# Staging x1's first half inside the attention loop and joining attention and mixing in one block (GLA and pooling trunk, one Trainium2 core)

## What is computed

```python
# layer 0: gated linear attention, 4 heads, chunks of 64 tokens
h = x @ w_in                      # q, k, v, g, low-rank gate
o = intra-chunk attention + q-decayed state of the chunks before
o = rmsnorm(o) * norm_w * silu(g)
x1 = layernorm(alpha * x + o @ w_out)
# layer 1: causal pooling mixer, width 2048, windows 2, 4, 8, 16
u, z = split(x1 @ w_in)
m = (windowed mean of u - u) @ w_grp + b, scaled
y = (m * silu(z)) @ w_out
out = layernorm(alpha * x1 + y)
```

## Time and profile before

| | |
|---|---|
| executions shown | 1974.26 us median of 3 (1969.22, 1974.26, 1974.47) |
| the profiled execution | 1964.6 us; its span 1962.9 us, 1.7 us lie around the span |
| mean granted clock | 0.981 |
| PE busy | 1861.6 us (95%) |
| PE weight loads | 1535.0 us (78%) |
| DVE busy | 1398.3 us (71%) |
| ACT busy | 852.5 us (43%) |
| POOL busy | 598.2 us (30%) |
| DMA | 171 GB/s over the span |

### The profile page before, as it was taken

One profiled execution on the slowest core, in us unless ns is written; L12 is line 12 of the kernel. 1 busy time (PEld: TensorE's weight loads), 2 busy tenths in 40 slices (PEclk: granted clock), 3 DMA queues, 4 the chain that ended last, 5 costly groups with the idle time before them and its releaser, 6 DMA issues.

```text
span 1962.9 us, 24653 instructions
## 1 busy us (share of the span) xinstructions
PE 1861.6 (95%) x8688; PEld 1535.0 (78%) x8688; DVE 1398.3 (71%) x1769; ACT 852.5 (43%) x1323; POOL 598.2 (30%) x380
## 2 busy tenths in 40 slices
PE   8989999999999699999679999999999998999997
PEld 7878887886788588888558888887888786887786
DVE  3454555778667678787666788768899967546997
ACT  4554445657555434333444444344333344224221
POOL 1322231332221000000145665405566532323330
PEclk9999999999999799999879999999999999999999
DMA  8967572557365645443413544242546326556442
GB/s 286 321 200 266 195 248 97 152 141 247 90 171 179 239 145 188 171 162 138 171 43 116 170 150 144 98 172 75 178 170 221 140 93 215 208 192 257 161 151 97
DMA packets 259725, 336.43 MB, mean 171 GB/s; under 512 B 18208, under 2 KB 187936, under 8 KB 255904
## 3 DMA queue, kind: packets, MB, share of 16 engines
q1 hardware_dynamic: 259616, 335.02, 50.9%
HBM read 218.58 MB, written 116.39 MB: 171 GB/s over the span
## 4 chain that ended last, share of the span: by engine, by line
PE 38%; DVE 7%; issue 4%; ACT 1%; POOL 0%; DVEq 0%; ACTq 0%; POOLq 0%
PE banks L200 13%; PE banks L202 12%; PE banks L201 12%; DVE m_w_lo L2520 2%; DVE m_x_lo L2534 1%; DVE m_win_a L2550 1%; ACT m_x_hi L2310 0%; DVE m_res L2633 0%; DVE m_win_b L2550 0%; DVE m_x_lo L2512 0%; PE banks L2203 0%; PE banks L2250 0%; DVE m_win_b L2566 0%; DVE m_res L2617 0%; DVE m_x_lo L2494 0%
## 5 line engine op out<-in xcount | busy, mean ns | idle before, releaser
L200 PE MATMUL banks<-m_x_hi,m_w_hi 128*128 128x512 f32 x1320 | 517.7, 392 | 12.6 <-DVE m_z L2596 6.6
L201 PE MATMUL banks<-m_x_lo,m_w_hi 128*128 128x512 f32 x1320 | 515.1, 390 | 0.0
L202 PE MATMUL banks<-m_x_hi,m_w_lo 128*128 128x512 f32 x1320 | 514.9, 390 | 0.0
L200 PEld LDWEIGHTS banks<-m_x_hi,m_w_hi 128*128 128x128 f32 x1320 | 248.8, 188 | 68.7 <-DVE m_w_lo L2520 10.6
L202 PEld LDWEIGHTS banks<-m_x_hi,m_w_lo 128*128 128x128 f32 x1320 | 248.7, 188 | 52.1
L201 PEld LDWEIGHTS banks<-m_x_lo,m_w_hi 128*128 128x128 f32 x1320 | 248.6, 188 | 51.8 <-issue 0.7
L200 PE MATMUL banks<-b_hi,h_w_hi 128*128 128x512 f32 x656 | 257.9, 393 | 6.1 <-issue 4.5
L202 PE MATMUL banks<-b_hi,h_w_lo 128*128 128x512 f32 x656 | 256.3, 391 | 0.0
L201 PE MATMUL banks<-b_lo,h_w_hi 128*128 128x512 f32 x656 | 256.0, 390 | 0.0
L2298 ACT ACTIVATE m_w_hi<-m_s 128x512 fp32r<-128x512 f32 x184 | 115.5, 629 | 186.2 <-PE banks L202 166.0
L2436 POOL TENSOR_TENSOR m_s<-pair_raw 128x512 f32<-128x512 f32 x24 | 46.7, 1945 | 469.0 <-POOLq L1512 365.1
(11 more groups left out here) (276 smaller groups left out, 3363.2 us busy)
## 6 DMA issues: line engine op xcount, KB each, us to landing
b_raw<-x_in SPq DMA_DIRECT2D x14, 1024.0 KB, 9.8
p_in<-in_pool_w_in SPq DMA_DIRECT2D x32, 256.0 KB, 5.7
w_fused<-p_out SPq DMA_DIRECT2D x32, 256.0 KB, 3.5
x_in<-h_terms SPq DMA_DIRECT2D x8, 1024.0 KB, 4.3
v_tiles<-h_v_out SPq DMA_DIRECT2D x16, 512.0 KB, 4.0
in_raw<-in_gla_w_in SPq DMA_DIRECT2D x16, 512.0 KB, 5.3
h_raw<-in_gla_w_in SPq DMA_DIRECT2D x16, 512.0 KB, 5.9
k<-k_tiles SPq DMA_DIRECT2D x32, 256.0 KB, 4.2
```

The source lines that it names most:

```text
L200: nc.tensor.matmul(out, a_hi, b_hi, start=first, stop=False, skip_group_check=True)
L201: nc.tensor.matmul(out, a_hi, b_lo, start=False, stop=False, skip_group_check=True)
L202: return nc.tensor.matmul(out, a_lo, b_hi, start=False, stop=last, skip_group_check=True)
```

## The change

1. **Staging in attention.** The hardware loop ends at t = 7; steps 8 to 17 are written out. In steps 8 to 15 a chunk c = t - 8 of x1's first half is staged, as the second half is later: SP loads 256 KB of x1's rows into `a_stage_rows` at the head of the step (r = 0) and again behind `load_qkv` (r = 1, into the same buffer, behind the first turning); PE turns four 128x128 blocks behind the outputs and four behind the second half of y, both into `sum_ps`, the bank of `mean`; ACT copies them out, r = 0 behind the squares, r = 1 in the next step behind `norm_scale`; POOL makes the four sums and **issues the seven stores itself**. `load_qkv` now stands ahead of `load_x`.
2. **One block.** Attention and mixing share an `nc.Block`, with no barrier between. The prologue of mixing is gone. Step 0 is treated as an epoch's first step: terms loaded from `x_terms[0]`, split by `turn_hi(0, n)` and `turn_lo(0, n)`, two products native. The last residual and norm of attention stand between these.
3. **The edge to `project`.** Four stores of the last gates and two loads of w_out rows go from `project`'s end to the start of the new block.

```diff
+            if staged(c):
+                load_stage_rows(c, pair, s, 0)
             if lag >= 1 and not (static and t + 1 >= NT):
                 sp.wait_ge(gated_done, t)
                 load_g(t + 1, 1 - s)
             if has(t, lag, TAIL):
                 sp.wait_ge(out_done, (t - TAIL) * 2 + 2)
                 sp.dma_start(p.x1[ds((t - TAIL) * P, P), :], out[1 - s][:]).then_inc(out_stored[1 - s], DMA)
-            if lag >= LAG and not (static and t >= NT):
-                sp.wait_ge(y_read, (t - LAG) * 2 + 2)
-                load_x(t, s)
             if not (static and t + 2 >= NT):
                 sp.wait_ge(o_mm, t + 1)
                 p.load_qkv(sp, t + 2, s)
+            if staged(c):
+                load_stage_rows(c, pair, s, 1)
+            if lag >= LAG and not (static and t >= NT):
+                sp.wait_ge(y_read, (t - LAG) * 2 + 2)
+                load_x(t, s)
...
+        def load_stage_rows(c, pair, kk, r):
+            if r:
+                sp.wait_ge(st_turned, c * 2 + 1)
+            else:
+                if c:
+                    sp.wait_ge(st_turned, c * 2)
+                sp.wait_ge(out_stored[kk], (pair - 1) * DMA)
+                sp.wait_ge(out_stored[1 - kk], (pair + (kk - 2)) * DMA)
+            rows = p.x1[ds((pair + 4 * r - STAGED // 2) * P, P), :].rearrange("p (h c) -> p h c", h=2)
+            sp.dma_start(stage_rows[:], rows[:, :, kk * 2 * P:(kk + 1) * 2 * P]).then_inc(st_rows, DMA)
...
+        def turn_stage(t, c, r):
+            pe.wait_ge(st_rows, (c * 2 + (r + 1)) * DMA)
+            if r:
+                pe.wait_ge(st_copied, c * 2 + 1)
+            else:
+                pe.wait_ge(rms_mid, t)
+            for b in range(4):
+                last = nc.tensor.transpose(sum_ps[:, b * P:(b + 1) * P], stage_rows[:, b // 2, b % 2 * P:(b % 2 + 1) * P],
+                                           p.ident[:])
+            last.then_inc(st_turned, 1)
...
+        def copy_stage(c, r):
+            act.wait_ge(st_turned, c * 2 + (r + 1))
+            if c:
+                act.wait_ge(st_sum, c * 4)
+                act.wait_ge(st_stored, c * (PRODUCTS * DMA))
+            stage = stage_b if r else stage_a
+            nc.scalar.activation(stage[:].rearrange("p h k t -> p (h k t)"), sum_ps, ACT.Copy).then_inc(st_copied, 1)
...
+        for c in range(CHUNKS):
+            pool.wait_ge(st_copied, 2 * c + 2)
+            if c:
+                pool.wait_ge(st_stored, c * PRODUCTS * DMA)
+            nc.gpsimd.tensor_tensor(t1, b12, b11, ALU.subtract).then_inc(st_sum, 1)
...
+            for j, src in ((1, stage_a[:, 0, :, :]), (2, stage_a[:, 1, :, :]), (3, stage_b[:, 1, :, :]),
...
+                pool.dma_start(p.x_terms[0, j - 1, :, k:k + 2, cols], src).then_inc(st_stored, DMA)
...
+    def load_first(sp):
+        p.load_pair(sp, p.pair_raw0, TILES[0], 0)
+        for n, dst in enumerate((ahead[0], ahead[1], first_raw)):
+            sp.dma_start(dst[:], p.x_terms[0, ORDER[n] - 1]).then_inc(x_loaded[n], DMA)
...
-            for n in range(HT):
-                turn_first(n)
...
+        y_ended()
+        load_x(0, 3)
             load_pair(1)
+        load_x(0, 4)
+        load_x(0, 6)
+        store_last()
+        load_x(0, 5)
```

More of the change, by code:

```diff
@@ L1491, in attend_and_norm, with run @@
     LAG, TAIL = 2, 3
-    def run(engine, step):
+    STAGED = NT // 2
+    CHUNKS = NT // 2
+    def run(engine, step, end):
         for t in range(TAIL + 1):
             step(t, t % 2, min(t, TAIL), t // 2)
-        with engine.Fori((TAIL + 1) // 2, NT // 2 - 1) as pair:
+        with engine.Fori((TAIL + 1) // 2, STAGED // 2) as pair:
             for s in range(2):
                 step(pair * 2 + s, s, TAIL, pair)
-        for t in range(NT - 2, NT + TAIL):
-            step(t, t % 2, TAIL, t // 2)
+        for t in range(STAGED, end):
+            step(t, t % 2, TAIL, t // 2, t - STAGED)
     def has(t, lag, behind):
@@ L1831, in pool_mix_and_out @@
+    return sync, tensor, scalar, gpsimd, vector
+def pool_mix_and_out(nc, p, a, out_dram, phase):
     HALF = SEQ // 2
@@ L1864, in pool_mix_and_out @@
     rstd = [p.place(f"m_rstd{b}", [P, 1]) for b in range(2)]
+    assert p.at <= p.scores_at
+    p.at = p.scores_at
+    raw = [p.pair_raw0, p.place("m_pair_raw1", [P, 2 * KT, P])]
+    for j in (1, 5, 4):
+        place_w(j)
+    assert p.at <= p.kn_at
+    p.at = p.kn_at
+    for j in (1, 5):
+        place_hi(j)
+        place_lo(j)
+    carry = p.place("m_carry", [P, MT, PAD])
+    assert p.at <= p.qkv0_end
+    p.at = p.qkv0_end
+    place_hi(4)
+    place_lo(4)
+    assert p.at <= p.state_at
+    s1, s2, s3, s4 = (p.place(f"m_s{n}", [P, HALF_K, P]) for n in range(1, 5))
+    place_w(6)
     shared_at = p.at
@@ L1870, in pool_mix_and_out @@
     p.at = shared_at
-    first_a = [p.place(f"m_first_a{s}", [P, KT, P]) for s in range(2)]
-    first_b = [p.place(f"m_first_b{s}", [P, HALF_K, P]) for s in range(2)]
+    first_raw = p.place("m_first_raw", [P, HALF_K, BLK])
     p.at = shared_at
@@ L1931, in turns_to, with loaded @@
     def turns_to(e, n):
-        return PRODUCTS * (e - 1) + TURNS.index(n) + 1
+        return PRODUCTS * e + TURNS.index(n) + 1
+    def loaded(e, n):
+        if n < PRELOADED:
+            return ahead[n][:]
+        return first_raw[:] if (e, n) == (0, 2) else x_raw[ORDER[n]][:]
     def turning(turned, i, slot):
-        return [(epoch(i - later) + 1, n) for n, (later, at) in turned.items() if at == slot and follows(i - later)]
+        return [(LAST_OF_EPOCH.index(i - later), n) for n, (later, at) in turned.items()
+                if at == slot and i - later > 0 and follows(i - later)]
     def epoch(i):
-        return sum(i > last for last in LAST_OF_EPOCH)
+        return sum(i > last for last in LAST_OF_EPOCH) - 1
     def group(i):
```

1895 lines of the change are left out of this document (956 added, 939 removed).

## The result

The changed kernel takes **2001.98 us** (median of 4, 1997.23 to 2005.77) against 1973.7 (median of 4) for the kernel before: ratio 1.0147, 95% interval 1.0118 to 1.0176. It is slower by 28 us. The forecast was 1985 with a range of 1963 to 2010 and 0.55 on slower.

The account below looks back on a forecast made before the run. PE, busy for all 18.21 us of an attention step, bounds it. Attention +36.3, seam -25.0, edge -1.0 give +10.3: 1974.9 profiled, 1985 us as median once 9.7 is added; range 1963 to 2010, own range 1971 to 1997.

Parts of the forecast that it names:

- the rival of a slow issue by GpSimd: Staged attention steps: POOL's stores, not the loads, set the pace from D = 1.36; 2011 us at 1.6, chance 0.20.
- the signs of being wrong: Second turning starts without a stall, steps 8 to 15 take over 26 us each, or seam longer than 70 us.
- Transposes, 0.9 a step: Attention steps 8 to 15: eight added transposes on PE in each step, 0.9 us taken, 7.2 us in all.
- The rows queue behind q to v, a stall of 3.6 in six steps: Steps 8 to 13: second rows land 9.5 us after the outputs, PE wants them at 6.0; 21.6 us in all.
- The averaging's wait, 1.35: Attention: averaging matmuls wait for ACT's copy behind the scaling, hidden by PE stalls except in two steps; 2.7 us.
- The clock, 0.8 for each of six stalls: Attention: PE falls to 1.2 GHz after a stall, half of 1.6 us taken for each; 4.8 us (0 to 9.6).
- D: Time GpSimd needs to issue one store of a chunk: taken as 1.1 us, between 0.50 and 1.75.
- The stall from stores, 7D - 5.95: Staged steps: PE waits because stores must land before ACT copies the next chunk; 1.8 us, lying under the 3.6.
- The seam, -25.0: Attention to mixing: step 1 starts 61.7 us after E, the end of y in attention step 15, instead of 86.7.
- The edge, -1: Edge to `project`: moved loads and stores gain at most some of PE's wait there; -1 us (+2 to -5).
- The later stages are unchanged: Stages after the seam: no change in time, no term in the sum.
- The rival of loads in time: Attention: second rows do not queue behind v, leaving at most 1.35 us a step; 1966 us, chance 0.25.

Follow-up runs that it names:

- experiment 4: Changed kernel with the second row load ahead of q to v on SP and ACT's second-turning copy ahead of the scaling: 1954.11 us, ratio 0.9913.
- Experiment 1: Changed kernel with the second load of rows issued ahead of the loads of q to v on SP: 1969.54 us, ratio 0.9989.
- Experiment 2: Changed kernel with 12 unread matmuls put ahead of the second turning in steps 8 to 13: 1982.79 us, ratio 1.0048.
- Experiment 3: Changed kernel with the seven stores of a chunk issued by SP in the next step instead of by POOL: 2000.03 us, ratio 1.0147.
- experiment 8: experiment 4 with mixing's first buffer group also moved, so all x and weights start 64 bytes off a multiple of 128: 1950.09 us, ratio 0.9883.
- experiment 5: Kernel before the change with all SBUF buffers of mixing moved by 64 bytes: 1972.96 us, ratio 0.9997.
- 10: experiment 8 with the two loads of w_out rows behind the loads of tile 1's q to v: 1949.09 us, ratio 0.9884.
- 9: experiment 4 with the two loads of w_out rows behind the loads of tile 1's q to v: 1952.6 us, ratio 0.9896.
- experiment 7: experiment 4 with the weights of products 1, 5, 4, 6 and the buffers behind them on multiples of 128 bytes: 1955.38 us, ratio 0.9916.

## Why the prediction was right, and where it was off

The direction was right and the time lay in the range, but the forecast of 1985 was 17 us short: +10.3 us forecast, +28 measured. The time lies above the forecast's own range too (1971 to 1997). What carried the stated range to 2010 was the rival of a slow issue by GpSimd, and that rival was wrong; that the time lay in the stated range is luck. Of the signs of being wrong one came once, a step over 26 us (step 9, 26.4). Against the traces' +39.1 the forecast lacked 28.8: 12.7 in attention, 0.7 at the seam, 1.0 at the edge, 12.2 in mixing and 2.2 from project. Step by step:

- **Transposes, 0.9 a step: right.** 19.08 against 18.21 us in experiment 4, 0.87.
- **The rows queue behind q to v, a stall of 3.6 in six steps: right.** 19.0 us in six waits, 3.2 each, for 21.6. "From q's issue to v's is 2.2 us, and v lands 5.9 later", plus 0.8 and 0.6, gave 9.5 us from the outputs to the landing; in step 9 it was 8.7 from q's issue. (9.5 less 6.0 is 3.5; the forecast carried 3.6.) Experiment 1 takes away the order and with it the stall.
- **The averaging's wait, 1.35: right in being hidden, and in size where the stall is gone.** In the changed kernel it shows in the two last steps only, at 2.6 and 3.1 us (5.7 for 2.7 forecast, since no state update stands ahead of it there and PE asks sooner). In experiment 1 it is there in all eight, and lengthens a step by 20.53 - 19.08 = 1.45.
- **The clock, 0.8 for each of six stalls: the term that was mis-sized.** The forecast took half of one row's 1.6 us. The trace says: seven steps took 172.4 us; 7 x 19.08 (experiment 4) = 133.6 are work at full clock, 19.0 stalls, and the remaining 19.9 us are the clock, 3.3 for each stall. All six gaps of 2.8 to 3.5 us were followed by a fall, none was spared as after 468.74, and the slow stretch lasted 9.4 us behind the gap of step 8 and 6.7 behind that of step 9, over transposes, scores and the state update, where the forecast had eight matmuls. Experiment 2 confirms it from the other side. With 3.3 in place of 0.8 the sum would have been 15 us higher, 2000. That this is so near the measured 2002 is in part chance, since it still lacks the 6 us of the buffers' places below.
- **"D ... is in no row ... I take 1.1".** It is 0.72, near SP's end. The stall from stores, 7D - 5.95, is then below nothing: ACT's first copy did wait for the stores in four steps, 8.8 us in all, but in the three of them in which PE waited for rows it was done 5 us before these landed. Experiment 3 shows that the issuer does not matter. The rival of a slow issue was wrong. The Trainium skill (SBUF — State Buffer, "Who interferes with whom") has DVE lock GpSimd out of writing descriptors in its two-port operations, and infers that products of two tensors do not. Here DVE was in products and sums of two tensors during 37.7 of the 40.7 us that the 56 issues took, and 55 of them took 0.723 to 0.729 us; the trace agrees with the inference.
- **The seam, -25.0: right, at -24.3, by errors that cancel, which is luck.** The last store had landed and SP went on at E+17.1 for E+21.75: seven issues of 0.72 for 1.1 (2.7 less) and sums of 2.9 for 5.5 (2.6 less). From there to the first product it was 16.1 us for 14.4, and step 0 took 29.2 us for 25.5, with gaps of 1.25, 2.64 and 0.74 in it.
- **The edge, -1: nothing** between the two traces, 1 to 2 us at most over all of them, within the bounds given.
- **"The later stages are unchanged": wrong.** The instructions are, the time is not: 12.2 us more after step 1. Some 6 of it is 0.15 us a step from the buffers' places (experiment 8), which the change brings with it and which I took for bookkeeping. The rest is within what executions of the same stage differ by. From ACT's copy in mixing step 1 to the end the trace before has 939.9 us, and others with steps of 19.04 have 943.6 (experiment 5), 943.4 and 945.1 (8 and 10); the changed kernel has 952.1, and others with steps of 19.19 have 945.0 to 950.3 (1 to 4 and 9). The means, 943.0 and 949.0, are 6.0 apart, and the two traces compared lie at the ends. The 2.2 us from project are of the same kind: its last matmul starts at 636.95 before, and at 638.5 to 643.6 in all other traces.

The rival of loads in time, that transfers spread over all engines and so do not queue, fell: a DMA share of 0.5 averaged over a step said nothing of the 8 us in which q to v fly.

## What to carry to other kernels

A stall of PE costs what follows it too: price a recurring gap of some 3 us with the slow stretch behind it, and if it can't be removed, fill it. Before blaming the work that a change adds, look at which queue each new wait and DMA joins and what stands ahead of it: here the added transposes cost 7 us, a load's place in SP's queue 32, and a copy's place in ACT's 15. And after moving buffers, compare the length of a step that the change did not touch.

## What was not expected of the hardware

- **The place of buffers in SBUF changes a matmul's time by 3%.** Stationary weights (and the buffers behind them) moved by 64 bytes against the moving operand: starts 0.2333 us apart for 0.2267, in all 84 matmuls of a step; all moved together: nothing. No product was slow in the programs in which x and weights of all seven start at one and the same place in a multiple of 128 bytes (the kernel before, experiments 5, 8 and 10). The rule behind it is open. In the changed kernel only product 6 has x and weights at different places, and it takes 2.80 us for 2.72; but products 2 and 4, which have them at one place, take 2.75 and 2.76, and in experiment 7 product 6 is as slow with both on a multiple of 128. A product may also pay for standing at another place than the one ahead of it; no run separates the two.
- **The same four sums of 128x256 on POOL take 0.73 us each in attention and mostly 1.18 to 1.74 in mixing,** and the trace shows what goes with it. In attention they run beside nothing on DVE or beside operations that read one operand from PSUM (`a_state`, `a_gated`). In mixing they run beside DVE's sums of two operands in SBUF, as here:

```profile
1133.65 1.77 DVE L2626 TENSOR_TENSOR m_win_a<-m_win_b 128x1033 f32<-128x1033 f32 x1
...
1134.40 1.61 POOL L2562 TENSOR_TENSOR m_stage_t<-m_stage_a,m_stage_t 128x256 f32<-128x256 f32 x1
```

The last of the four took 0.74 in the two chunks in which nothing ran on DVE beside it, and 1.61 in the other six. No run tested it by an edit.

- **Useless matmuls in a stall made the program 19 us faster,** since they kept PE at 2.4 GHz (clock 1.00 in five of six steps).
